# Post-norm of a two-layer block on one core: Sqrt and reciprocal in place of Ln and Exp, the gate tiles' low parts in pieces, three side products in other PSUM banks

## The reference, cut to what matters

```python
for i in range(DEPTH):                                   # DEPTH = 2
    y = _even_layer(x, ...) if i % 2 == 0 else _conv_layer(x, ...)
    x = _layernorm(DEEPNORM_ALPHA * x + y, post_ln_g[i], post_ln_b[i])
    x = x + (p[i] @ ple_w[i]) * jax.nn.sigmoid(x @ ple_gate_w[i])
```

## Time and profile before

| | |
|---|---|
| median of 3 runs | 2159.27 us (2154.77 to 2161.27) |
| the profiled execution | 2159.29 us |
| its span in the trace | 2157.6 us |
| PE busy | 2125.5 us, 99% of the span |
| PE weight loads | 1736.4 us, 80% |
| DVE busy | 1239.9 us, 57% |
| ACT busy | 804.7 us, 37% |
| POOL busy | 341.7 us, 16% |
| granted PE clock, mean | 0.994 of 2.4 GHz |

### The profile page before, as it was taken

How to read it: one execution, slowest core, us unless ns; L and a number is a source line. 1 busy time by engine, 2 the same in 40 slices (tenths; PEclk the granted TensorE clock), 3 DMA queues, 4 the chain that set the end, 5 groups by cost and what they waited for, 6 DMA issues and landing times.

```text
span 2157.6 us, 28484 instructions
## 1 busy us (share of the span) xinstructions
PE 2125.5 (99%) x10434; PEld 1736.4 (80%) x10434; DVE 1239.9 (57%) x2102; ACT 804.7 (37%) x985; POOL 341.7 (16%) x179
## 2 busy tenths in 40 slices
PE   9999999999999999999899999999999999999998
PEld 8888878878888787888688788888888778886887
DVE  5224565664665756346633478888888763466332
ACT  4224354464553556122622322222323452126221
POOL 0000000000000000000400034444757420003000
PEclk9999999999999999999999999999999999999999
DMA  8222222222122123322133322222222234221331
GB/s 320 79 98 82 77 77 78 78 73 72 71 78 78 61 95 118 117 92 95 70 123 122 131 79 98 98 97 98 97 98 97 79 120 153 98 97 59 127 119 65
DMA packets 32818, 213.60 MB, mean 99 GB/s; under 512 B 3888, under 2 KB 3904, under 8 KB 9200
## 3 DMA queue, kind: packets, MB, share of 16 engines
q1 hardware_dynamic: 27936, 189.28, 24.8%
q0 software_dynamic: 4528, 22.99, 2.8%
q10 hardware_dynamic: 288, 0.52, 0.1%
HBM read 204.39 MB, written 8.39 MB: 99 GB/s over the span
## 4 chain that ended last, share of the span: by engine, by line
PE 95%; ACT 2%; DVE 2%; issue 1%; DMA 0%; POOL 0%; ACTq 0%; DVEq 0%; POOLq 0%
PE G L446 88%; PE X L446 5%; PE T L446 1%; PE T L589 1%; ACT w_hi L805 1%; ACT Y L1052 1%; DVE w_lo L1172 0%; ACT a_hi L809 0%; DVE a_lo L1177 0%; DMA Z<-xT_in 0%; POOL a_lo L367 0%; PE T L700 0%; DVE tmp L1546 0%; ACT Z L989 0%; DVE Y L1575 0%
## 5 line engine op out<-in xcount | busy, mean ns | idle before, releaser
L446 PE MATMUL G<-a_hi,w_hi 128*128 128x512 f32 (+1 forms) x2784 | 1093.1, 393 | 19.4 <-POOL a_lo L367 10.6
L446 PE MATMUL G<-a_lo,w_hi 128*128 128x512 f32 (+1 forms) x2784 | 1081.8, 389 | 0.0
L446 PE MATMUL G<-a_hi,w_lo 128*128 128x512 f32 x2752 | 1074.4, 390 | 0.0
L805 ACT ACTIVATE w_hi<-w_raw 128x2048 fp32r<-128x2048 f32 x174 | 333.2, 1915 | 1077.2 <-PE G L446 1071.8
L1172 DVE TENSOR_TENSOR w_lo<-w_raw,w_hi 128x2048 fp32r<-128x2048 f32 x127 | 291.1, 2292 | 672.6 <-ACT w_hi L805 672.4
L446 PEld LDWEIGHTS G<-a_hi,w_hi 128*128 128x128 f32 x2784 | 524.4, 188 | 138.5 <-POOL a_lo L367 16.2
L446 PEld LDWEIGHTS G<-a_lo,w_hi 128*128 128x128 f32 x2784 | 524.9, 189 | 107.3 <-issue 1.5
L446 PEld LDWEIGHTS G<-a_hi,w_lo 128*128 128x128 f32 x2752 | 518.3, 188 | 109.5
L1712 DVE SCALAR_TENSOR_TENSOR T<-tmp,par,T 128x512 f32<-128x512 f32 x464 | 306.9, 748 | 0.0
L390 POOL TENSOR_TENSOR w_lo<-w_raw,w_hi 128x2048 fp32r<-128x2048 f32 x46 | 212.5, 4618 | 249.5 <-ACT w_hi L805 249.5
L361 POOL DMA_DIRECT2D Y<-xT_in x4 | 2.1, 533 | 825.1 <-DVE a_lo L1177 825.1
(11 more groups left out here) (232 smaller groups left out, 1474.4 us busy)
## 6 DMA issues: line engine op xcount, KB each, us to landing
w_raw<-wall_in SPq DMA_DIRECT2D x174, 1024.0 KB, 4.8
Y<-w_in POOLq DMA_DIRECT2D x2, 2048.0 KB, 17.5
Y<-xT_in POOLq DMA_DIRECT2D x4, 1024.0 KB, 5.1
x_residual<-Y POOLq DMA_DIRECT2D x16, 256.0 KB, 3.8
Y<-x_residual POOLq DMA_DIRECT2D x4, 1024.0 KB, 5.2
out<-Y POOLq DMA_DIRECT2D x16, 256.0 KB, 3.6
w_raw<-wall_in SPq DMA_DIRECT2D x12, 256.0 KB, 7.7
Z<-xT_in SPq DMA_DIRECT2D x6, 512.0 KB, 9.3
```

Of the source, the lines that this page charges most:

```text
L446: return pe.matmul(o, l, r, start=start, stop=stop)
L805: f(w_hi[:, w.slot, :], w_raw[:, w.slot, :], ACT.Copy).then_inc(S("w_hi"), 1)
```

## The change

It touches both post-norms. On ACT, Ln and Exp give way to one Sqrt, whose table is loaded ahead by an instruction of its own on a few columns of ones (`load_root_table`), and DVE takes the reciprocal. On DVE, `w_lo` of gate tile 0 is made in two halves behind chunks 2 and 4, and that of gate tile 1 in four quarters behind chunks 5 to 8; ACT makes `w_hi` of gate tile 1 in quarters too, and PE waits for parts. On PE, both spreads stand one side product earlier, the second gate tile follows the first by four chunks and at the end by one (`GATE_LAG`), and side products 5 to 7 go into the banks T0, T1 and X0, from which ACT copies them only after the last chunk. The numbers of the `G` banks behind it shift by three per layer.

```diff
+GATE_LAG = (4,) * 8 + (3,) * 4 + (2,) * 2 + (1,) * 2
+LATE = 5
+        LATE_BANKS = (TB[0], TB[1], X[0])
...
-            def gemm_pair(w, g, acts, between=None, quarters=False):
+            def gemm_pair(w, g, acts, between=None, quarters=False, parts=None):
...
-                for k in range(KC + LAG):
-                    lag = START_LAG[k] if quarters and k < KC else LAG
+                lags = START_LAG if quarters else GATE_LAG if parts else (LAG,) * KC
+                for k in range(KC + lags[-1]):
+                    lag = lags[min(k, KC - 1)]
...
+                        elif parts and kn % (8, 4)[n] == 0:
+                            if kn == 0:
+                                pe.wait_ge(S(f"bank_free{gn.slot}"), gn.half())
+                            if kn + (8, 4)[n] < KC:
+                                pe.wait_ge(S("part_split"), parts + n + kn // 4)
+                            else:
+                                pe.wait_ge(S("w_split"), wn.n(1))
...
-                ple_pack(layer, 1, range(2, 4))
+                ple_pack(layer, 1, range(2, 3))
                 spread_mean(n, diag_d)
-                ple_pack(layer, 1, range(4, 5))
+                ple_pack(layer, 1, range(3, 4))
                 spread_dev(n)
-                ple_pack(layer, 1, range(5, 8))
+                ple_pack(layer, 1, range(4, 8))
                 w, g = W_GATE[layer], G_GATE[layer]
-                gemm_pair(w, g, f"x1_split{layer}")
+                gemm_pair(w, g, f"x1_split{layer}", parts=10 + 4 * layer)
...
+            def load_root_table():
+
+                f(stat[:, 3 * NT:4 * NT], ones[:, 0:NT], ACT.Sqrt)
+
             def deviation(n):
...
-                f(dev, var, ACT.Ln).then_inc(S("ln_log"), 1)
-                act.wait_ge(*after("ln_log", n, 1))
-                f(dev, dev, ACT.Exp, scale=-0.5).then_inc(S("ln_guess"), 1)
+                f(dev, var, ACT.Sqrt).then_inc(S("ln_root"), 1)
...
                     elif j < 3:
                         x1_high(j)
-                        ple_out(layer, 1, j + 5)
-                    if j == 6:
-                        split(Idx(w + 18))
+                    if 3 <= j and j < 7:
+                        if j == 3:
+                            act.wait_ge(S("gemm_done"), w + 17)
+                            act.wait_ge(*landed(Idx(w + 18)))
+                        f(w_hi[:, 0, quarter(j - 3)], w_raw[:, 0, quarter(j - 3)], ACT.Copy).then_inc(
+                            S("w_hi" if j == 6 else "quarter_hi"), 1)
                 x1_high(KC - 1)
+                for c in range(LATE, 8):
+                    ple_out(layer, 1, c)
...
-                if between:
-                    between()
-
+                dve.wait_ge(*after("ln_root", n, 1))
+                dve.reciprocal(dev, dev).then_inc(S("ln_guess"), 1)
...
-                statistics(n_ln, diag_d, lambda: split(Idx(w + 17)))
+                statistics(n_ln, diag_d)
...
-                    if j == 9:
-                        split(Idx(w + 18))
+                    if j in (2, 4):
+                        split_part(Idx(w + 17), j // 4, 2, 10 + 4 * layer)
+                    if 5 <= j and j < 9:
+                        split_part(Idx(w + 18), j - 5, 4, 11 + 4 * layer)
```

More of the change, by code:

```diff
@@ L56 @@
 W_TILES = 177
[L58 to L61, removed]
+G_PLE = ((61, 85), (154, 178))
+G_OUT = (69, 162)
+G_GATE = (90, 183)
+G_CONV = 106
+LATE = 5
 HALVES = (64, 32, 16, 8)
@@ L117 @@
     half_summed=4, shift_done=1, shift_ready=1, sums_set=3, centred=16, c_summed=16, squared=16, sq_summed=16, mean_sum=1,
-    var_sum=1, ln_step=6, var=1, ln_log=1, ln_guess=1, diag_d=1, diag_r=1, mean_spread=1, dev_spread=1, less_mean=16, normed=16)
+    var_sum=1, ln_step=6, var=1, ln_root=1, ln_guess=1, diag_d=1, diag_r=1, mean_spread=1, dev_spread=1, less_mean=16, normed=16)
 class Idx:
@@ L335, in _ @@
             for q in range(4):
-                sp.wait_ge(*((S("quarter_split"), 2 * q + 1) if q < 3 else (S("w_split"), 1)))
+                sp.wait_ge(*((S("part_split"), 2 * q + 1) if q < 3 else (S("w_split"), 1)))
                 sp.dma_start(w_raw[:, 0, quarter(q)], wall[2][:, quarter(q)]).then_inc(S(quarter_landed(0, q)), 16)
@@ L483, in gemm_pair @@
                         if quarters and kn % 4 == 0:
-                            pe.wait_ge(*((S("quarter_split"), kn // 2 + n + 1) if kn < 12 else (S("w_split"), n + 1)))
+                            pe.wait_ge(*((S("part_split"), kn // 2 + n + 1) if kn < 12 else (S("w_split"), n + 1)))
+                        elif parts and kn % (8, 4)[n] == 0:
[5 more added lines that the diff above has]
+                                pe.wait_ge(S("w_split"), wn.n(1))
                         elif kn == 0:
@@ L512, in ple_pack @@
                         pe.wait_ge(S("p_split"), layer + 1)
-                    g = Idx(G_PLE[layer][u] + c)
-                    pe.wait_ge(S(f"bank_free{g.slot}"), g.half())
-                    o = G[g.slot][:, :]
+                    if u == 1 and c >= LATE:
+                        o = LATE_BANKS[c - LATE][:, :]
+                    else:
+                        g = Idx(G_PLE[layer][u] + c)
+                        pe.wait_ge(S(f"bank_free{g.slot}"), g.half())
+                        o = G[g.slot][:, :]
                     for k in range(PLE_K):
@@ L988, in ple_out @@
                     act.wait_ge(S("ple_done"), 14 * layer + 7 * u + c + 1)
-                frees(f(chunk(Z, 8 * u + c), G[g.slot][:, :], ACT.Copy), g)
+                if u == 1 and c >= LATE:
+                    f(chunk(Z, 8 * u + c), LATE_BANKS[c - LATE][:, :], ACT.Copy)
+                else:
+                    frees(f(chunk(Z, 8 * u + c), G[g.slot][:, :], ACT.Copy), g)
             prev_hz(HEADS, Idx(W_PLE[0][0] - 1))
@@ L1036, in second_part @@
                             square(n_ln, i * 4 + c, ln_sq[c % 2], i * 4 + (c - 1))
+                load_root_table()
                 split(Idx(w + 17))
@@ L1205, in split_quarter @@
                 tt(w_lo[:, n, quarter(q)], w_raw[:, n, quarter(q)], w_hi[:, n, quarter(q)].bitcast(F), ALU.subtract).then_inc(
-                    S("w_split" if q == 3 else "quarter_split"), 1)
+                    S("w_split" if q == 3 else "part_split"), 1)
             for q in range(4):
@@ L1539, in add_last, with statistics @@
                 tt(sqs, sqs, sq, ALU.add).then_inc(S("sq_summed"), 1)
-            def statistics(n, diag_of_mean, between=None):
+            def statistics(n, diag_of_mean):
                 mean, off, var, dev, rr = [stat[:, k * NT:(k + 1) * NT] for k in range(5)]
@@ L1584, in second_part, with split_part @@
                 n_ln = 2 * layer
+                def split_part(w, q, parts, n_parts):
+                    at = slice(q * D // parts, (q + 1) * D // parts)
+                    last = q == parts - 1
+                    dve.wait_ge(*((S("w_hi"), w.n(1)) if last or parts == 2 else (S("quarter_hi"), 10 + 3 * layer + q)))
+                    tt(w_lo[:, w.slot, at], w_raw[:, w.slot, at], w_hi[:, w.slot, at].bitcast(F), ALU.subtract).then_inc(
+                        S("w_split" if last else "part_split"), 1)
                 def out_chunk(w, g, j):
```

## The result

| | before | after |
|---|---|---|
| median of 20 runs | 2158.93 us (2154.77 to 2161.27) | 2161.74 us (2160.84 to 2165.32) |
| ratio after/before | | 1.0018 (95%: 1.0011 to 1.0024) |
| the profiled execution | 2159.29 us | 2162.25 us |
| its span | 2157.6 us | 2160.6 us |
| transition, first layer | 46.48 us | 47.09 us |

A transition is the time from the start of the last output matmul to the start of gate tile 2's first. The change made the kernel slower by 0.18%: clear of noise by its interval, but within the 0.3% of "no change". The forecast was 2162.5. The transitions and the last row are each read from one traced execution.

What follows compares the result with a forecast made beforehand. PE, busy for 99% of the span, was taken to bound the kernel. Transitions of +0.5 and -0.55 us, together nothing, plus 3.2 for low clock on the profiled 2159.29 gave 2162.5 us, own range 2158 to 2165.7.

Steps and rivals of the forecast that it cites:

- The statistics: Post-norm's Sqrt and reciprocal (0.2 us): diagonal ready 2 us earlier, `spread_dev` and DVE's first division 1.40 earlier.
- ACT's copy of product 4: On ACT's list ahead of chunk 0, it gives most back: chunk 0's gain and bias only 0.25 us earlier.
- The chain: Chunks through ACT, DVE and POOL in the gate pair: `a_lo` of chunk 8 at 82.0, 15 at 90.7; no earlier overall.
- the rule: DVE and POOL exclude each other when both read two SBUF operands; each piece holds or awaits `a_lo`, up to 1.25 us.
- The sum: Both transitions: +0.5 us in the first layer, -0.55 in the second, together nothing; low clock adds 3.2.
- Rival 1: Gate pairs: same plan without DVE and POOL collisions, at full clock; -1.4 and -2.5 us, 2155.4 us; chance 0.13.
- The banks: Three free banks ahead of the pair remove PE's waits for copies, some 0.5 us; costed at nothing.
- Behind the pair: Gate tile 2 starts 4.78 us after gate tile 0's last matmul, at 98.84, after 3.2 us of PE idling.
- The clock: PE at 1.2 GHz for one stretch per transition, +1.6 us each, +3.2 in all.
- Rival 3: Slower: clock falls after both holes of each transition, 4.4 us each, 8.8 in all, 2168.1 us; chance 0.19.
- Rival 2: Faster: clock stays up, chain 1.4 us early, pair's end covered; -3.4 and -4.5 us, 2151.4 us; chance 0.07.
- Rival 4: Gate pair: pieces late, PE waits for gate tile 1's `w_lo`; costs nothing, forecast's time; shares the forecast's 0.61.

Runs made afterwards that it cites:

- lnexp: Changed kernel with Ln and Exp back in place of the square root, its early table load and the reciprocal: 2163.17 us.
- copy4: Changed kernel with ACT's copy of side product 4 behind chunk 0's gain, bias and high part instead of ahead: 2160.55 us.
- psum: Changed kernel with the `w_lo` pieces of gate tiles 0 and 1 reading a PSUM bank in place of `w_raw`: 2159.48 us.
- early: Changed kernel with both halves of gate tile 0's `w_lo` right behind the diagonal, lags as changed: 2160.53 us.
- both_early: Changed kernel with lags growing 4 to 6, gate tile 0's `w_lo` halves behind the diagonal, product 4's copy behind chunk 0, mean two chunks ahead: 2149.24 us.
- banks: Changed kernel with side products 5 to 7 back in banks `G0` and `G1` and their ACT copies between chunks: 2162.84 us.
- b_lag: Kernel before with only the changed kernel's gate-pair lags (4, then 3, 2, 1): 2166.70 us, ratio 1.0038 to before.
- both_early_ln: `both_early` with Ln and Exp in place of the square root and reciprocal: 2152.02 us.

## Why the prediction was right

**The statistics.** Right. The first division starts at 9.52 behind the reference (before 10.94), 1.42 earlier for 1.40. The reciprocal took 0.17 for the 0.2 of the estimate. The prediction doesn't divide the 2 us by which the diagonal comes earlier; `lnexp` gives the root 1.1 of them, and 0.9 belongs to moving the `w_lo` of 2.28. Of the 1.42, `lnexp` keeps 0.98 (its first division is at 9.96), so the root gives 0.44 of it and the rest comes from the lists: the place of the spread and of that `w_lo`.

**ACT's copy of product 4.** Right. Chunk 0 starts at 11.43 (before 11.66), 0.23 earlier for 0.25, and `copy4` shows that the copy held it.

**The chain.** Right. Chunk 8's `a_lo` ends at 30.0 (forecast 30.2) and chunk 15's at 38.8 (38.9). Pieces were stretched as forecast, to 2.24 and 0.95, and one of POOL's chunks to 2.16. One reading behind the rule was off: in the earlier trace rows DVE's 4.04 didn't end with POOL's 4.63 but 0.55 us later, so the loser does nearly all of its own 0.68 behind the winner. The sum didn't use the difference. Rival 1 had gate tile 2 at 96.9 without collisions, 1.9 before the forecast's 98.84; `psum`, which has none, gains 1.6 in each layer. The stretching and its price are shown; the rival's "short pieces find the other engine free" fell.

**The banks.** Costed at nothing, and they are worth 0.5 us per transition. I looked at PE's waits for copies; what counts, as I read it, is that ACT, with 1.2 to 1.4 us of work for each chunk, has no room for three copies. The sum stood because in the chain that I put together the copies were already gone.

**Behind the pair.** Right, and this was the step that decided the sign: forecast an idle time of 3.2 and gate tile 2 at 47.0, measured 3.11 and 47.09 and 47.11.

**The clock.** Right in the sum by luck, wrong in the places and in the size. I took one stretch per transition at 1.6 each, 3.2. There was one in each pair, in which PE was waiting for chunks much of the time and which moved the forecast end by at most 0.1 (in `psum` the first pair has such a stretch and the second has none, and the copies start at 41.13 and 41.12). And there was one of 6.8 us behind the second pair only, which cost 2.9. Nothing in the forecast says why that is one pair and not both; with both it would have been 3.4 to 4.7, as in the traces of `psum` and `lnexp`. The median ended 0.8 below the forecast. Rival 3 has the right mechanism for what did happen behind the pair, at 8.8 us in all; here it cost 2.9, and in `lnexp`, where the clock fell behind both pairs, 1.8 and 2.9.

**Rival 2**, that the end of the pair is covered, fell with the 3.11. **Rival 4** did not occur: no wait of PE in the pair names the pieces.

## What to carry to other kernels

When two streams share an engine with a lag, the lag at the end is the cover for whatever has to be reloaded when the first one finishes: size it by that chain (here 4.78 us, seven units), and shorten it only where the holes are, at the start. A gain on one engine is worth what the next item in the next engine's list lets through; the square root was worth 0 us behind a copy of 0.5 us that stood ahead of its user, and 1.1 once that copy was gone and DVE had other work in its idle time. Put subtractions with two SBUF operands on DVE where GpSimd is idle, or give them a PSUM operand.

## What the runs showed of the hardware

**The clock behind a short idle time.** Fourteen gate pairs in seven kernels ended with PE idle for 3.11 us. At twelve of them the granted clock fell to 1.2 GHz, late in the idle time or up to 1.5 us behind it, for 3.4 or 6.8 us; in these traces it did so at none of the fourteen pairs of the other seven. The rest of the span prices it: 158.2 or 158.3 us with no fall behind the second pair, 159.9 or 160.0 with 3.4 us, 161.1 with 6.8 us, so 1.7 and 2.9 us. That comes on top of the 3.11 of idling. The price is half of what lies behind gate tile 2's start: nearly all of the 3.4 us, but only 5.8 to 6.0 of the 6.8. Inside a pair, where PE waits for chunks, a stretch costs less: nothing that shows for 3.4 us in `psum`, 0.7 more for 6.8 than for 3.4 us in `early` and 0.1 more in `copy4`, and 1.1 more for 10.2 us than for 3.4 in the kernel before. Where the chain was earliest (`both_early`), neither pair had any stretch at 1.2 GHz, inside or behind it. Behind the second pair of `banks` the clock stayed up after the same idle time:

```profile
1998.00:2001.40 3.40, 0.58 (x3) 0.51 (x4) 2.89 (x2) 3.37 (x4) 0.00 (x0) 1.00 0.00 0
2001.40:2004.80 3.40, 3.40 (x17) 2.79 (x16) 3.39 (x3) 1.16 (x2) 0.58 (x1) 1.00 0.84 299
```

These are windows of `banks` (columns as in the earlier trace rows): 0.58 us of work in 3.4, and then full clock. In `b_lag`, 1.30 us in the same length were followed by 1.2 GHz:

```profile
2004.10:2007.50 3.40, 1.30 (x6) 1.09 (x7) 3.27 (x4) 3.39 (x4) 0.00 (x0) 1.00 0.20 34
2007.50:2010.90 3.40, 3.40 (x10) 2.63 (x9) 3.28 (x3) 0.44 (x1) 0.58 (x1) 0.51 0.86 341
```

The windows were laid by hand, though, and the picture depends on it. Cut at 1999.60, the same idle time of `banks` is divided into two windows, with 1.50 and 2.19 us of work:

```profile
1996.20:1999.60 3.40, 1.50 (x7) 0.93 (x5) 1.21 (x1) 3.14 (x2) 0.00 (x0) 1.00 0.01 2
1999.60:2003.00 3.40, 2.19 (x10) 1.81 (x11) 3.27 (x4) 2.95 (x4) 0.02 (x1) 1.00 0.29 70
```

So the 0.58 doesn't show that less work is safe. What tells the two apart, the runs don't settle.

**Two table loads for Ln and Exp.** `lnexp`, `both_early_ln` and the kernel before load a table ahead of each, 1.28 us every time, and in the post-norms the Ln or Exp follows its load's end by 0.01 or 0.02 us.
